# A hybrid attention and mixture-of-experts block: another order of work in the odd mixer, GpSimd adds, and a later first gather

## The reference

```
def odd_mixer(a_lat, a_ctx, ...):                 # layer 1
    p = (a @ w_in).reshape(b, n, 8, 4 * 64 + 128) # per head: q1 q2 k1 k2 v
    lam = exp(sum(lam_q1 * lam_k1)) - exp(sum(lam_q2 * lam_k2)) + lam_init
    q1, q2, k1, k2 = apply_rope(...)              # latent tokens only: x*cos + rot(x)*sin
    a1, a2 = softmax(q1 k1), softmax(q2 k2)       # keys: context and latent
    o = (a1 - lam * a2) @ v
    return (rmsnorm(o, g_sub) * (1 - lam_init)) @ w_out

def routed_experts(xf, top_idx, top_w, w_gate, w_up, w_down):
    for tok, w, e in blocks_of_128_slots:
        xb = x_pad[tok]
        h = silu(xb @ w_gate[e]) * (xb @ w_up[e])
        acc = acc.at[tok].add((h @ w_down[e]) * w[:, None])
```

## Time and profile before

| | before |
|---|---|
| median of 3 runs | 3107.07 us (3100.58 to 3112.63) |
| the profiled execution: its own time | 3107.07 us |
| its span, first to last instruction | 3105.3 us |
| mean granted TensorE clock | 0.944 of full |
| busy: TensorE, VectorE, ScalarE, GpSimd | 2736.1, 1725.1, 1462.1, 991.4 us |

### The profile page before, as it was taken

How to read it: one execution, slowest core, us unless ns; L and a number is a source line. 1 busy time by engine, 2 the same in 40 slices (tenths; PEclk the granted TensorE clock), 3 DMA queues, 4 the chain that set the end, 5 groups by cost and what they waited for, 6 DMA issues and landing times. The chain is left out here.

```text
span 3105.3 us, 37707 instructions
## 1 busy us (share of the span) xinstructions
PE 2736.1 (88%) x12450; PEld 1942.5 (63%) x12450; DVE 1725.1 (56%) x2132; ACT 1462.1 (47%) x2059; POOL 991.4 (32%) x697
## 2 busy tenths in 40 slices
PE   7979999987879999999994679997779999999990
PEld 2345677775457676666772668885547677667660
DVE  7923244543745555656563855555465566565546
ACT  5612233431146666666662344444126666666650
POOL 1000000012345555555551000001235555555542
PEclk9989999998989999999997789998889999999995
DMA  9930100023059999999995611102329999999966
GB/s 349 354 119 14 41 1 1 1 78 151 6 208 379 386 387 370 375 373 375 382 340 190 250 55 37 37 11 85 149 76 367 374 365 342 362 348 346 358 251 257
DMA packets 160999, 694.89 MB, mean 224 GB/s; under 512 B 34776, under 2 KB 46040, under 8 KB 100752
## 3 DMA queue, kind: packets, MB, share of 16 engines
q1 hardware_dynamic: 116240, 607.41, 52.0%
q0 software_dynamic: 43520, 84.21, 7.1%
q10 hardware_dynamic: 1152, 2.11, 0.2%
HBM read 678.82 MB, written 86.08 MB: 246 GB/s over the span
## 5 line engine op out<-in xcount | busy, mean ns | idle before, releaser
L1571 DVE TENSOR_TENSOR F_gu_lo<-gu_raw,F_gu_hi 128x2048 fp32r<-128x2048 f32 x292 | 662.2, 2291 | 589.3 <-ACT F_gu_hi L1516 580.3
L1516 ACT ACTIVATE F_gu_hi<-gu_raw 128x2048 fp32r<-128x2048 f32 x292 | 554.2, 1918 | 71.8 <-DMA gu_raw<-in_we_up_dram 47.7
L1465 PE MATMUL F_psY<-d_raw,F_hT 128*128 128x512 f32 x1168 | 525.6, 593 | 2.9 <-ACT F_hT L1534 2.9
L102 PE MATMUL F_psG<-F_gu_hi,F_xT_hi 128*128 128x512 f32 x1168 | 470.5, 403 | 6.9 <-DVE F_xT_lo L1563 6.9
L104 PE MATMUL F_psG<-F_gu_hi,F_xT_lo 128*128 128x512 f32 x1168 | 458.0, 392 | 0.0
L103 PE MATMUL F_psG<-F_gu_lo,F_xT_hi 128*128 128x512 f32 x1168 | 456.5, 391 | 0.0
L1391 POOL DMA_INDIRECT F_xb<-f_d,F_gi x146 | 339.4, 2325 | 130.5 <-POOL F_gi L1388 120.5
L1465 PEld LDWEIGHTS F_psY<-d_raw,F_hT 128*128 128x128 f32 x1168 | 211.2, 191 | 212.9 <-issue 209.5
L1530 ACT ACTIVATE F_yb<-F_psY,wgt 128x1024 f32<-128x1024 f32 x146 | 163.1, 1117 | 362.2 <-PE F_psY L1465 362.2
L1388 POOL COPY F_gi<-gat 128x1 int32 (+1 forms) x146 | 303.4, 2078 | 15.4 <-PE F_psX L1448 15.1
L102 PEld LDWEIGHTS F_psG<-F_gu_hi,F_xT_hi 128*128 128x128 f32 x1168 | 221.7, 190 | 49.2 <-DVE F_xT_lo L1563 8.3
(11 more groups left out here) (335 smaller groups left out, 4430.3 us busy)
## 6 DMA issues: line engine op xcount, KB each, us to landing
gu_raw<-in_we_gate_dram SPq DMA_DIRECT2D x146, 1024.0 KB, 9.0
gu_raw<-in_we_up_dram SPq DMA_DIRECT2D x146, 1024.0 KB
d_raw<-in_we_down_dram SPq DMA_DIRECT2D x146, 1024.0 KB, 6.9
wada<-in_w_ada_dram SPq DMA_DIRECT2D x24, 2048.0 KB, 11.2
I_ring<-y_d SPq DMA_DIRECT2D x24, 1024.0 KB, 7.0
H_y<-y_d SPq DMA_DIRECT2D x4, 4096.0 KB, 18.9
I_w_raw<-in_wc_in_dram SPq DMA_DIRECT2D x32, 384.0 KB, 3.3
f_d<-D_f SPq DMA_DIRECT2D x10, 512.0 KB, 2.6
```

The lines of the kernel that those rows point to most:

```text
L102: nc.tensor.matmul(acc, xh, wh, start=(start and i == 0), stop=False)
L1465: ins = nc.tensor.matmul(psY[:, n], hT[:, j, k], d_raw[:, j, k, c], start=(k == 0), stop=(k == KF - 1))
L1516: nc.scalar.activation(gu_hi[:, j, v], gu_raw[:, j, v], ACT.Copy).then_inc(s_guh, 1)
L1571: V.tensor_tensor(gu_lo[:, j, v], gu_raw[:, j, v], gu_hi[:, j, v].bitcast(F32), ALU.subtract).then_inc(s_gul, 1)
```

## The change

1. In an expert stage GpSimd clears all four buffers and issues both dummy scatters before gathers 0 and 1. Before, each of these gathers stood right behind the clearing of its own buffer.
2. In the odd mixer SyncE issues the first two weight pieces first, then three row transfers, then the other two pieces of head 0, and lambda's vectors after them. VectorE and ScalarE split all of head 0 before anything else, and head 1 in the first tile.
3. TensorE turns tile t at the head of its own step, and no longer between the products of the tile before.
4. VectorE does both rotations of a step behind the first sums, and all of the last sums, the residual and the low part after them. ScalarE's order changes with it.
5. The add that ends a rotation (a copy, for context tiles) goes from VectorE to GpSimd (`added`), also for the 36 rotations inside the attention units. VectorE now waits for `s_qk` before it writes the two products again, and GpSimd for `s_tr`.

```diff
@@ stage_experts, GpSimd
                         for j in range(2):
                             G.memset(xb[:, j], 0.0).then_inc(s_xb0, 1)
-                            pool.wait_ge(s_xb0, j + 1)
-                            gather(j, j)
-                        for j in range(2):
                             G.memset(yb[:, j], 0.0).then_inc(s_xb0, 1)
                             G.tensor_copy(si[j][:], moe.sca[:, TBL - 1:TBL]).then_inc(s_si, 1)
...
                         for j in range(2):
                             send(j)
+                        gather(0, 0)
+                        gather(1, 1)
@@ stage_mix1, SyncE
+                        weights(0, range(0, RAW))
+                        for g in range(RING):
+                            rows(g)
+                        weights(0, range(RAW, WS))
                         for n, name in enumerate(("lam_q1", "lam_k1", "lam_q2", "lam_k2")):
                             sp.dma_start(lamv[:, n], ...).then_inc(s_lam, 16)
-                        for g in range(RING):
-                            rows(g)
-                        weights(0, range(0, RAW))
-                        for g in range(RING, RING + 3):
-                            rows(g)
-                        weights(0, range(RAW, WS))
+                        rows(3)
                         weights(1, range(0, RAW))
-                        for g in range(RING + 3, RING + 6):
+                        for g in range(4, 6):
                             rows(g)
                         weights(1, range(RAW, WS))
-                        for g in range(RING + 6, 4 * NT):
+                        for g in range(6, 4 * NT):
                             rows(g)
@@ stage_mix1, TensorE
-                        turn_rows(0)
                         for t in range(NT):
+                            turn_rows(t)
                             project(0, t)
                             if t >= 1:
                                 turn_qk(1, t - 1, 0)
-                            if t + 1 < NT:
-                                turn_rows(t + 1)
                             project(1, t)
                             turn_qk(0, t, 0)
@@ stage_mix1, VectorE
                             if n >= 2:
-                                dve.wait_ge(s_tr, n - 1)
+                                dve.wait_ge(s_qk, n - 1)
...
-                                link(ins, s_prd)
-                                V.tensor_tensor(qk[:, n % 2], t1[:, n % 2], t2[:, n % 2], ALU.add).then_inc(s_qk, 1)
                             else:
-                                ins = V.tensor_copy(qk[:, n % 2, 2:4], product_of(n)...)
-                                link(ins, s_prd)
-                                dve.sem_inc(s_qk, 1)
+                                ins = V.tensor_copy(t1[:, n % 2, 2:4], product_of(n)...)
+                            link(ins, s_prd)
...
+                        for i in range(WS):
+                            split_low(0, i)
                         dve.wait_ge(s_lam, 64)
...
                             if t < NT:
                                 sum_first(t)
+                            if t >= 3:
+                                rotate(1, t - 3)
+                            if 2 <= t < NT + 2:
+                                rotate(0, t - 2)
                             if 1 <= t < NT + 1:
                                 normed(t - 1)
-                            if t >= 3:
-                                rotate(1, t - 3)
                             if t < NT:
-                                sum_last(t, 2)
-                            if 2 <= t < NT + 2:
-                                rotate(0, t - 2)
-                            if t < NT:
-                                sum_last(t, 3)
-                                residual(t)
-                            if t < EARLY:
+                                sum_last(t)
+                            if t == 0:
                                 for i in range(WS):
-                                    split_low(t, i)
+                                    split_low(1, i)
@@ stage_mix1, GpSimd
+                        def added(hd, s):
+                            n = number(hd, s)
+                            pool.wait_ge(s_prd, n + 1)
+                            if n >= 2:
+                                pool.wait_ge(s_tr, n - 1)
+                            if s < NL:
+                                G.tensor_tensor(qk[:, n % 2], t1[:, n % 2], t2[:, n % 2], ALU.add).then_inc(s_qk, 1)
+                            else:
+                                G.tensor_copy(qk[:, n % 2, 2:4], t1[:, n % 2, 2:4]).then_inc(s_qk, 1)
@@ stage_mix1, ScalarE
-                        act.wait_ge(s_lamd, 1)
-                        nc.scalar.activation(lam2[:], lam2[:], ACT.Exp).then_inc(s_lame, 1)
-                        for t in range(NT + 3):
-                            if 1 <= t < NT + 1:
-                                squares(t - 1)
+                        for hd in range(EARLY):
+                            for i in range(WS):
+                                split_high(hd, i)
+                            if hd == 0:
+                                act.wait_ge(s_lamd, 1)
+                                nc.scalar.activation(lam2[:], lam2[:], ACT.Exp).then_inc(s_lame, 1)
+                        for t in range(1, NT + 3):
                             if t >= 3:
                                 copy_v(1, t - 3)
+                            if t < NT + 1:
+                                squares(t - 1)
                             if 2 <= t < NT + 2:
                                 copy_v(0, t - 2)
                             if 3 <= t < NT + 2:
                                 copy_qk(1, t - 3)
-                            if t < EARLY:
-                                for i in range(WS):
-                                    split_high(t, i)
-                            if 1 <= t < NT + 1:
-                                high(t - 1)
                             if 2 <= t < NT + 2:
                                 copy_qk(0, t - 2)
+                            if t < NT + 1:
+                                high(t - 1)
```

More of the change, by code:

```diff
@@ L1946, in sum_first, with sum_last @@
                             dve.wait_ge(s_yf, 4 * t + 2)
[L1948 to L1954, removed]
+                        def sum_last(t):
+                            for i in (2, 3):
+                                y = arrived(4 * t + i)
+                                link(V.tensor_tensor(y[:, 0], y[:, 0], y[:, 1], ALU.add))
+                                V.tensor_tensor(ac, ac, y[:, 0], ALU.add).then_inc(s_yf, 1)
+                                dve.wait_ge(s_yf, 4 * t + i + 1)
                             if t == 0:
@@ L1985, in rotate @@
                                     ins = V.tensor_tensor(t4[:, :, :, w], s4[:, :, :, 1 - w], n4[:, :, :, w], ALU.mult)
-                                link(ins, s_prd)
-                                V.tensor_tensor(qk[:, n % 2], t1[:, n % 2], t2[:, n % 2], ALU.add).then_inc(s_qk, 1)
-                            else:
-                                ins = V.tensor_copy(qk[:, n % 2, 2:4], product_of(n)[:, 2 * DHALF:4 * DHALF].rearrange("p (g d) -> p g d", d=DHALF))
-                                link(ins, s_prd)
-                                dve.sem_inc(s_qk, 1)
+                            else:
+                                ins = V.tensor_copy(t1[:, n % 2, 2:4], product_of(n)[:, 2 * DHALF:4 * DHALF].rearrange("p (g d) -> p g d", d=DHALF))
+                            link(ins, s_prd)
                         def maximum(u):
@@ L2064, in _ @@
                         G = nc.gpsimd
+                        def added(hd, s):
[8 more added lines that the diff above has]
+                        for t in range(1, NT + 3):
+                            if t >= 3:
+                                added(1, t - 3)
+                            if 2 <= t < NT + 2:
+                                added(0, t - 2)
+                        for u, fresh in steps:
+                            for hd, s in fresh:
+                                added(hd, s)
                         pool.wait_ge(s_rec, 1)
```

## The result

| | before | after |
|---|---|---|
| median | 3107.0 us (3100.58 to 3112.63, 4 runs) | 3136.88 us (3134.22 to 3140.2, 4 runs) |
| the profiled execution: its own time | 3107.07 us | 3145.33 us |
| its span | 3105.3 us | 3143.5 us |
| mean granted TensorE clock | 0.944 | 0.942 |

The kernel became slower: the ratio is 1.0097, with a 95% interval of 1.0076 to 1.0119, or 29.9 us. The forecast was 38.6 us later, with a range of 20 to 53 us later. The profiled execution of after lies 8.4 us above the median of after, so the stages are compared by their lengths within a trace, and the medians are compared apart.

The account below looks back on a forecast made before the run. It took VectorE to bound the mixer's tile building and TensorE its attention units. Expert starts, mixer start, tile cycle and clock summed 12.4 - 3.3 + 21.9 + 7.6 = 38.6 us later, 3145.7 us, range 3127 to 3160.

Parts of the forecast that it names:

- Expert stages, 12.4: Start of both expert stages: first gather issued 6.2 us later behind memsets and scatters, twice, 12.4 us slower.
- The lower bound, 8.4: Expert starts: with fewer weight transfers beside it, a gather's landing could save 2 us each, leaving 8.4 in all.
- Rival (b): Expert stages: gathers land behind the scatters' data, +10 us, 3156 us; chance 0.09.
- Mixer start, -3.3: Odd mixer's start: new order of transfers and splits brings the first product 3.3 us earlier, bounds -10 to +5.
- The tile cycle, +21.9: Mixer tiles: nothing covers the turn's evacuation, so one chain makes a tile 19.8 us against 15.2; +21.9 us in all.
- Rival (d): Mixer tiles: chain shorter than counted, so VectorE sets the cycle at 14.5 us; +5.6 in all, 3113 us; chance 0.06.
- The clock, +7.6: Mixer tiles: TensorE's clock falls to 1.2 GHz after each 5.8 us gap, slowing the products; +7.6 us in all.
- rival (a): Mixer: TensorE's clock stays at 2.4 GHz, so 31.0 us later in all, 3138 us; chance 0.20.
- Attention units, 0: Attention units: TensorE is the bound and its work is the same, so 0 us, bounds -4 to +5.
- Rival (c): Mixer: GpSimd blocks VectorE, each of 32 adds holding the path by 0.7 us; +22, 3168 us; chance 0.04.
- Rival (e): Mixer start: first product much earlier, at best 21 us more gain; +17 in all, 3124 us; chance 0.05.

Follow-up runs that it names:

- e9: Kernel before with the new expert start, but gathers 0 and 1 behind all four memsets and ahead of both dummy scatters: 3111.5 us in one run.
- e7: Kernel before with the new mixer start alone (order of transfers, splits and lambda): 3102.42 us against 3108.24, ratio 0.9988.
- e5: e2 with 24 extra matmuls per tile, from the second on, behind TensorE's turn, their results unread: 3113.12 us in one run.
- e3: Kernel before with only TensorE's loop changed, turning tile t at the head of its own step: 3134.77 us, ratio 1.0087.
- e4b: e4 with ScalarE's old order too, evacuating the turn before copying head 0's transposes: 3112.12 us, ratio 1.0018.
- e6: Kernel before with the rotations' adds and copies on GpSimd everywhere, VectorE's order unchanged: 3113.65 us in one run.
- e2: Changed kernel with the expert stages' start put back as before, so the mixer's part alone: 3134.34 us, ratio 1.0083.
- e8: Kernel before with the new mixer start and the rotations' adds on GpSimd everywhere: median 3104.04 us, ratio 0.9995.
- e10: Kernel before with the new mixer start and the adds on GpSimd in the attention units only: 3103.39 us against 3109.74, ratio 0.9986.
- e4: e2 with TensorE's old loop put back, ScalarE's order still changed: 3140.5 us in one run.
- e1: Kernel before with the new expert start alone (gathers behind four memsets and two dummy scatters): 3115.12 us against 3106.49, ratio 1.0028.

## Why the prediction was right, and where its terms were off

The direction, the mechanism and the range held. The terms, in its own order:

**1. Expert stages, 12.4: measured 7.0.** The gather's issue ended 5.6 us later from the first memset (10.8 against 5.2) where 6.2 was counted; the first scatter's issue took 2.13 us, not 3.1. The step that failed is that TensorE starts 5.3 us after the gather whatever stands before it: it was 3.2, since here the scatter was the stage's first indirect transfer. The lower bound, 8.4, had the effect but not its cause, and was still too high. Rival (b), gathers behind the scatters' data, is refuted by the earlier trace rows against after's 3.2 us and by e9.

**2. Mixer start, -3.3: measured -6.2, -5.1 in e7, and -4.6 in the mean of all traces,** inside the bounds of -10 to +5. The step that was off is that pieces 2 and 3 come "near 1692.5", 19.6 us after the stage's first transfer: in after ScalarE has them at 1698.76, 16.9 us after that transfer (1681.87). The 2.7 us are kept to the end: the first product stands at 56.6 instead of 59.5. The rest of the sequence ran nearly as summed, with VectorE's waits of 2.22 and 1.88 us for the two row transfers.

**3. The tile cycle, +21.9: measured +19.4 with the clock held up (e5).** A middle cycle is 19.38 us where 19.8 was summed. The first (19.61 against 20.5) and the last (15.49 against 15.8) are also a little short. The chain is shown by e3. Rival (d), a chain shorter than VectorE's own cycle, is refuted. VectorE's busy time did fall to 14.2 to 14.5 us a cycle where the adds ran undisturbed (e4b, after), but in e6, where they collided with its sums, it was 14.97 and the cycle 16.4 to 16.5.

**4. The clock, +7.6: measured 7.3** (e2 against e5): 1.1 in each middle cycle and 2.2 in the context tile's, as summed, 0.4 in the first cycle, where nothing was counted, and 1.4 behind the last tile, where 2.2 was. The gap was 5.33 us and was followed by 1.2 GHz every time, as the step assumed; rival (a) is refuted by the row at 1778.61. Behind the waits of about 1 us in the earlier trace rows and e5 head 0's products began at 2.4 GHz. But the 0.89 that the prediction held against (a) came from another place, the product behind the turn at 1776.06, so it said nothing of a long gap. That the assumption held is partly luck. The Trainium skill ("TensorE: Matmul & The Clock Gate", section "HAM oscillation — how this bites in real kernels") says that a wait which recurs in every tile can make every tile start at the slow clock. This trace agrees for the wait of 5.33 us.

**5. Attention units, 0: measured -1.6 in after,** inside -4 to +5. The eight traces with the adds on GpSimd there show 296.2 to 299.5 us, the five without 298.5 to 298.7. The three among them that keep before's order in the tiles (e6, e8, e10) are all low, 296.2 to 296.9, but e2, e4, e4b and e5 are not, and no median is clear of noise: whether the adds gain anything here is left open. Rival (c) doesn't hold for after: its adds fall where VectorE is idle or has a small instruction (0.66 instead of 0.29 at 1786.43), with 3.25 us of slack behind. In the tiles in before's order it is real, as e6 shows. Rival (e), a much earlier first product, is refuted: the gain was 6.2.

**The sum.** After's mixer is 18.7 us longer and the two expert starts 7.0: 25.7 us. The medians differ by 29.9, with an interval of 23.6 to 37. The forecast, 38.6, is 8.7 above the medians and just outside that interval, and closer than its terms were, for errors of both signs met; the gather's term accounts for 5.4 of it, the start for 2.9, the tile cycle for 2.5 and the attention for 1.6, and against them stand about 4 us that the traces have in the expert stages beyond their starts. In the three traces with the late gather these stages last 810.9 to 816.3 and 758.8 to 764.6 us, in the ten others 805.7 to 811.5 and 752.2 to 762.6: 4.2 and 5.4 longer in the mean, 9.6 together instead of 7.0. The groups overlap, so that whether a late start makes later gathers wait more is left open. The profiled execution of after is at the top of both; its page has 54.4 us of TensorE's waits for gathers (L1447), the kernel before 38.3, e1 48.0. Its 8.4 us above the median may lie there; the runs of the median have no trace.

## What to carry to other kernels

Before an instruction is moved in one engine's stream, write down which work of that engine lies over what the instruction releases on the others. The turn was cheap between two products because ScalarE's evacuation and VectorE's remainder ran under the second one; with the same instructions one place later they cost 5.2 us a tile, 1.1 of it through the clock's fall. Such an order belongs to all engines together: taking it back on TensorE alone cost more than leaving it.

## What the runs showed that I had not expected

- The first indirect transfer of an expert stage takes 2.1 to 3.1 us to issue where later ones take 1.0 (in e9 2.07 us stood on the index copy ahead of it instead), and TensorE starts on the rows that it gathers 4.8 to 5.3 us after its issue, against 3.1 to 3.3 where a scatter was the first.
- A 128x256 add on GpSimd takes 0.73 us alone and 1.77 where VectorE had just begun a sum with two SBUF inputs; VectorE's next sum takes 1.63 instead of 1.22.
- A gap of 5.33 us behind 16 small matmuls was followed by a product at 1.2 GHz in every tile. With 24 matmuls in the gap, and 1.17 us of idle, it stayed at 2.4 GHz. Yet one product of before began at 1.2 GHz right behind its turn, with no wait above 1.11 us in its cycle.
